# Short products ahead of groups of products in a two-part model on one core

## The reference

```python
# first block, for each layer l
x = layer_norm(ALPHA * x + 0.5 * swiglu(x, ffn_w1[l, 0], ffn_w2[l, 0]), ...)
x = layer_norm(ALPHA * x + hybrid_mixer(x, ...), ...)
x = layer_norm(ALPHA * x + 0.5 * swiglu(x, ffn_w1[l, 1], ffn_w2[l, 1]), ...)

def swiglu(x, w1, w2):             # w1: 1024 x 5632, w2: 2816 x 1024
    g, u = jnp.split(x @ w1, 2, axis=-1)
    return (jax.nn.silu(g) * u) @ w2

# second block: layer 0 is the even mixer (long convolution and attention),
# layer 1 the odd mixer: 8 recurrent heads (mLSTM) over 256 rows and 256 rows of context
q, k, v, o, z, gates = _split(h @ w_in, ODD_SPLITS)    # of each head: q, k 128 wide; v, o, z 256 wide
h = (h_f + h_b) * jax.nn.sigmoid(o)                    # a forward and a backward recurrence
return (rms_norm(h) * jax.nn.silu(z)) @ w_out
```

## Time and profile before

| | |
|---|---|
| median of 3 runs | 2158.39 us (2155.07 to 2162.65) |
| the profiled execution | 2157.61 us, span 2155.8 us |
| PE busy | 2124.5 us |
| DVE, ACT busy | 1428.7 us, 902.1 us |
| mean granted TensorE clock | 0.997 |

### The profile page before, as it was taken

The page is one execution under the profiler, slowest core; times in us unless marked ns, Lnnn a source line. Parts: engine busy times, 40 slices in busy tenths (PEclk is TensorE's granted clock), DMA queues, the critical chain, the costliest instruction groups (busy, mean ns, idle before and its releaser), DMA issues.

```text
span 2155.8 us, 35428 instructions
## 1 busy us (share of the span) xinstructions
PE 2124.5 (99%) x14996; PEld 1928.7 (89%) x14996; DVE 1428.7 (66%) x2066; ACT 902.1 (42%) x1066; POOL 18.7 (1%) x36
## 2 busy tenths in 40 slices
PE   9999999999999999999999999999999989999998
PEld 8998999999989989999899768888788879999996
DVE  5556878675566558876756767777666447665665
ACT  4343466344344434474434352222444344443442
POOL 0000000000000000000000000000000000000000
PEclk9999999999999999999999999999999999999999
DMA  9644555666566555555575422222212232332331
GB/s 363 225 178 190 196 196 215 235 235 254 196 265 234 190 190 196 196 196 215 196 247 216 177 80 79 79 79 79 79 40 79 88 117 79 118 118 79 118 118 59
DMA packets 29006, 349.56 MB, mean 162 GB/s; under 512 B 2993, under 2 KB 5425, under 8 KB 8369
## 3 DMA queue, kind: packets, MB, share of 16 engines
q1 hardware_dynamic: 24672, 313.42, 39.6%
q0 software_dynamic: 4176, 33.89, 4.1%
HBM read 346.24 MB, written 1.05 MB: 161 GB/s over the span
## 4 chain that ended last, share of the span: by engine, by line
PE 94%; DVE 2%; ACT 2%; DVEq 1%; ACTq 0%; issue 0%
PE banks L922 13%; PE banks L780 12%; PE banks L775 12%; PE banks L776 12%; PE banks L1009 8%; PE banks L1087 6%; PE banks L1084 6%; PE banks L1083 6%; PE banks L792 3%; PE banks L1101 2%; PE banks L1097 2%; PE banks L1098 2%; PE banks L1278 2%; PE banks L1277 2%; PE banks L1279 2%; PE banks L878 1%
## 5 line engine op out<-in xcount | busy, mean ns | idle before, releaser
L2101 DVE TENSOR_TENSOR w_lo<-ring,w_hi 128x2048 fp32r<-128x2048 f32 x290 | 661.9, 2289 | 391.7 <-ACT w_hi L1515 388.1
L1515 ACT ACTIVATE w_hi<-ring 128x2048 fp32r<-128x2048 f32 x290 | 555.9, 1918 | 675.6 <-PE banks L780 445.2
L775 PE MATMUL banks<-x_hi,w_hi 128*128 128x256 f32 x2112 | 497.0, 278 | 0.5 <-ACT w_hi L1515 0.5
L776 PE MATMUL banks<-x_lo,w_hi 128*128 128x256 f32 x2112 | 495.7, 277 | 0.0
L775 PEld LDWEIGHTS banks<-x_hi,w_hi 128*128 128x128 f32 x2112 | 397.2, 188 | 1.5 <-issue 1.5
L776 PEld LDWEIGHTS banks<-x_lo,w_hi 128*128 128x128 f32 x2112 | 397.3, 188 | 0.0
L780 PE MATMUL banks<-x_hi,w_lo 128*128 128x256 f32 x2112 | 284.6, 277 | 1.0 <-DVE w_lo L2101 1.0
L780 PEld LDWEIGHTS banks<-x_hi,w_lo 128*128 128x128 f32 x2112 | 260.7, 188 | 1.4 <-DVE w_lo L2101 1.4
L1083 PE MATMUL banks<-x_hi,w_hi 128*128 128x512 f32 (+1 forms) x656 | 232.7, 368 | 0.0
L1084 PE MATMUL banks<-x_lo,w_hi 128*128 128x512 f32 (+1 forms) x656 | 225.8, 358 | 0.0
L1552 ACT ACTIVATE arena<-banks 128x512 f32<-128x512 f32 (+5 forms) x178 | 79.7, 471 | 284.5 <-PE banks L1087 164.7
(11 more groups left out here) (378 smaller groups left out, 2806.0 us busy)
## 6 DMA issues: line engine op xcount, KB each, us to landing
ring<-weights SPq DMA_DIRECT2D x147, 2048.0 KB, 7.8
arena<-mods POOLq DMA_DIRECT2D x11, 2048.0 KB, 11.4
bcast<-lnrows POOLq DMA_DIRECT2D x12, 512.0 KB, 5.1
ring<-weights SPq DMA_DIRECT2D x2, 1024.0 KB, 9.9
filt_sb<-filt POOLq DMA_DIRECT2D x2, 609.0 KB, 22.4
xrow<-x SPq DMA_DIRECT2D x1, 1024.0 KB, 5.2
arena<-hy_consts POOLq DMA_DIRECT2D x1, 1024.0 KB, 13.0
xrow<-ctx_rows POOLq DMA_DIRECT2D x1, 1024.0 KB, 6.8
```

The costliest lines, as they stand in the source:

```text
L775: nc.tensor.matmul(out, hi[:, k, t * P:(t + 1) * P], x_h[:, k, :], start=k == 0, stop=False)
L776: nc.tensor.matmul(out, hi[:, k, t * P:(t + 1) * P], x_l[:, k, :], start=False, stop=False)
L1515: nc.scalar.activation(hi, raw, ACT.Copy).then_inc(w_hi_done, 1)
L2101: v.tensor_tensor(lo, raw, hi.bitcast(F32), ALU.subtract).then_inc(w_lo_done, 1)
```

## The change

`columns_half`, `tile_r`, `pair`, `value_tile` and `output_gates` get a number of columns, `first` (or `leads`, one for each side). Where it isn't 0, `lead` issues one product of the group's first stationary tile with the first columns of its first moving tile, into the place that the group then overwrites with `start=True`. It adds nothing to any result. It stands behind the group's waits for its bank and its high weights. There are 42: 8 in pairs 7 to 10 of the up stage (0, 0), 20 in pairs 1 to 10 of (1, 1), 7 ahead of the first of four value tiles (of heads 1 to 7) and 7 ahead of the first of two output gates (heads 1 to 7), of 8 to 256 columns each.

```diff
--- before.py
+++ after.py
@@ -133,6 +133,11 @@
 MOD_SETS = ((0,), (1, 2), (3,), (4,), (5, 6), (7,), (8, 9), (10,), (11,))
 MOD_SLOT = (0, 1, 0, 0, 0, 1, 0, 0, 1, 0, 0)
 MOD_BLOCK = {key[2]: n for key, n in BLOCK_OF.items() if key[1] == "mod"}
+UP_LEADS = {(0, 0, 7): (64, 128), (0, 0, 8): (192, 256), (0, 0, 9): (64, 128), (0, 0, 10): (192, 256)}
+UP_LEADS.update({(1, 1, j): (32 * j - 32 + 16, 32 * j) for j in range(1, 9)})
+UP_LEADS.update({(1, 1, 9): (8, 24), (1, 1, 10): (40, 56)})
+VALUE_LEADS = (32, 64, 96, 128, 160, 192, 256)
+GATE_LEADS = (0, 64, 128, 192, 256, 32, 96, 160)
 MOD_AT = 4
 FIRST_BANKS = (5, 6)
 FIRST_HALVES = HALF_OF[DEPTH, "hy", 0, 0]
@@ -762,13 +767,19 @@
                 else:
                     released(pe, (split - 1) // 3, "layer", "turn", (split - 1) % 3, b)
 
-            def columns_half(l, x_h, x_l, *key):
+            def lead(out, stationary, moving, n):
+
+                nc.tensor.matmul(out[:, 0:n], stationary, moving[:, 0:n], start=True, stop=True)
+
+            def columns_half(l, x_h, x_l, *key, first=0):
 
 
                 h = HALF_OF[(l,) + key]
                 b = take(pe, l, "layer", *key)
                 _, hi, lo = half_views(h)
                 hi_ready(h)
+                if first:
+                    lead(banks[:, b, 0:SEQ], hi[:, 0, 0:P], x_h[:, 0, :], first)
                 for t in range(2):
                     out = banks[:, b, t * SEQ:(t + 1) * SEQ]
                     for k in range(KT):
@@ -830,12 +841,12 @@
                         low_features(side, False)
                         low_weights(side, True)
 
-            def pair(l, x_h, x_l, *key, split=None):
+            def pair(l, x_h, x_l, *key, split=None, leads=(0, 0)):
                 if split is not None:
                     first_pair(l, x_h, x_l, *key, split=split)
                     return
                 for side in range(2):
-                    columns_half(l, x_h, x_l, *key, side)
+                    columns_half(l, x_h, x_l, *key, side, first=leads[side])
 
             def gates(l):
 
@@ -983,7 +994,8 @@
 
             def ffn(l, f):
                 for j in range(FJ):
-                    pair(l, x_hi, x_lo, "up", f, j, split=None if j else l * 3 + 2 * f)
+                    pair(l, x_hi, x_lo, "up", f, j, split=None if j else l * 3 + 2 * f,
+                         leads=UP_LEADS.get((l, f, j), (0, 0)))
                     if j == 0 and l + f:
                         mod_columns(MOD_GROUPS.index((l, "turn", 1) if f else (l - 1, "turn", 2)))
                     if (l, "up", f) in MOD_GROUPS:
@@ -1087,12 +1099,14 @@
                     mm = nc.tensor.matmul(out, lo[:, k, part_], x2_hi[:, k, cols_], start=False, stop=k == KT - 1)
                 return mm
 
-            def tile_r(out, h, r):
+            def tile_r(out, h, r, first=0):
 
 
                 _, hi, lo = half_views(h)
                 rows_ = slice(r * P, (r + 1) * P)
                 hi_ready(h)
+                if first:
+                    lead(out, x2_hi[:, 0, rows_], hi[:, 0, :], first)
                 for k in range(KT):
                     nc.tensor.matmul(out, x2_hi[:, k, rows_], hi[:, k, :], start=k == 0, stop=False)
                     nc.tensor.matmul(out, x2_lo[:, k, rows_], hi[:, k, :], start=False, stop=False)
@@ -1377,16 +1391,17 @@
                 b = take(pe, i, "ml", "k")
                 tile_t(banks[:, b, :], HALF_OF[DEPTH, "qkv", i, 0], 1).then_inc(full[b], 1)
 
-            def value_tile(i, r):
+            def value_tile(i, r, first=0):
                 b = take(pe, i, "ml", "v", r // 2) if r % 2 == 0 else plan["ml"]["v", r // 2][0]
-                mm = tile_r(banks[:, b, (r % 2) * 256:(r % 2 + 1) * 256], HALF_OF[DEPTH, "qkv", i, 1], r)
+                mm = tile_r(banks[:, b, (r % 2) * 256:(r % 2 + 1) * 256], HALF_OF[DEPTH, "qkv", i, 1], r, first)
                 if r % 2:
                     mm.then_inc(full[b], 1)
 
-            def output_gates(i):
+            def output_gates(i, first=0):
                 b = take(pe, i, "ml", "o")
                 for r in range(RT):
-                    mm = tile_r(banks[:, b, r * ML_V:(r + 1) * ML_V], HALF_OF[DEPTH, "oz", i, 0], r)
+                    mm = tile_r(banks[:, b, r * ML_V:(r + 1) * ML_V], HALF_OF[DEPTH, "oz", i, 0], r,
+                                first if r == 0 else 0)
                 mm.then_inc(full[b], 1)
                 b = take(pe, i, "ml", "z")
                 for t in range(2):
@@ -1433,7 +1448,7 @@
 
             for i in range(ML_HEADS):
                 if i:
-                    output_gates(i)
+                    output_gates(i, GATE_LEADS[i])
 
                 b = take(pe, i, "ml", "mb")
                 for d, c0 in ((0, SEQ), (1, 0)):
@@ -1470,7 +1485,7 @@
 
                 if i + 1 < ML_HEADS:
                     for r in range(4):
-                        value_tile(i + 1, r)
+                        value_tile(i + 1, r, 0 if r else VALUE_LEADS[i])
                 else:
                     odd_half(0, 1)
                     odd_half(1, 0)
```

## The result

The changed kernel takes 2166.57 us (median of 10 runs, 2162.51 to 2170.32) against 2158.33 us before (10 runs): 8.2 us more, ratio 1.0041 (95% interval 1.003 to 1.0052). A second set of 12 runs gave 1.0026 (1.001 to 1.0043). The forecast was 2158, with a range from 2152 to 2166. Both intervals exclude no change.

What follows compares the result with a forecast made beforehand. The prediction took PE (TensorE), busy 2124.5 of 2155.8 us, as the bound. Leads cost 4.75 us, quicker pace returns 5.4: -0.6 us; 2157.61 - 0.6 + 0.8 = 2157.8, said as 2158, range 2152 to 2166.

Steps and rivals of the forecast that it cites:

- the lower end: Price of a lead read from one-column products (L1009), 101 ns each: 4.2 us for 42 leads.
- The plain-fp32 rival: At the leads: short products go at 1.69 ns a column, costing 8.2 us; 2166.6 without pace answer; chance 0.18.
- Which value I take: Pace behind leads: three quarters of column groups quicker, 5.4 us back, heads nothing; with 4.75 us cost, sum -0.6 us.
- its zero: Starting point: up stages (0, 0) and (1, 1) at 117.8 ns before the change; quicker pace would give 5.97 us.
- the 6 in 8: Column groups behind the transposes of `mod_columns`: a restart ends at the quicker pace in 6 of 8 cases.
- three quarters forecast: Column groups behind leads: three quarters at the quicker pace, 0.75 x (5.97 + 1.17) = 5.4 us given back.
- its 1.17 us: Down stage behind (0, 0): 60.43 us instead of 61.60 if the quicker pace comes, a gain of 1.17 us.
- 14 of 14: Recurrent heads: all 14 restarts of value tiles and output gates ended at the slower pace, so no gain was taken.
- no answer: Whole kernel: the pace does not respond to leads, so their 4.75 us stands in full, 2163.1 us; chance 0.27.

Runs made afterwards that it cites:

- all_256: The changed kernel with all 42 leads made 256 columns wide, the width of the products behind them; 2164.59 us, ratio 1.0029.
- only_00: The changed kernel with only the eight leads of up stage (0, 0), all other leads 0; 2161.70 us, ratio 1.0007.
- pin_64: The kernel before plus thirteen leads of 64 columns, only where stretches of column groups begin; 2178.62 us, ratio 1.0084.
- pin_columns: The kernel before plus eight leads behind `mod_columns`, 64 columns at (0, 0) pair 7 and 16 elsewhere; 2159.00 us against 2157.88, ratio 1.0004.
- same_again: The kernel before, run again without an edit; 2162.35 us, ratio 1.0005.

## Why the prediction was wrong

**What held.** No wait swallows a lead. Its price is one slot at every width from 8 to 256 columns: 0.113 us was forecast, 0.114 to 0.12 measured in `all_256`, and the distances behind narrower leads add up to the same. (The eight one-column records from which the lower end was read are four products, two records each as in the earlier trace rows; the 101 ns are those of a record, and a lead is one record.) The plain-fp32 rival, whose 2166.6 is within 0.1 us of the result, is not what happened, and the agreement is luck: at its rate a lead of 192 columns would take some 320 ns, and it is 0.09 us from the lead to the next product. The pace does answer to leads, in column groups.

**The step that failed** is "Which value I take", in two terms. The larger one is its zero, 4.6 us (45.31, 61.69 and 113.15 in the first trace against the means 44.47, 61.10 and 109.97 of the table below). The forecast took (0, 0) and (1, 1) of the one trace, both slow, for what the kernel does in every execution, and counted every quick group as a gain. They were two draws that had come out slow. The rows it rested on said so: six of eight restarts were quick, so on the average these stretches too should have been taken as mostly quick already. Ten traces now hold 68 such stretches without a lead behind the transposes; 10 of them are slow, all at four of the eight places ((0, 0) pair 7, (0, 1) pair 1, (1, 0) pair 7, (1, 1) pair 1). The forecast used the 6 in 8 for the changed kernel and not for the kernel before.

The smaller term is the share of quick groups behind leads, three quarters forecast and 10 of 28 found, in every traced execution the same ten: 10 x 0.21 = 2.1 us instead of 5.4, 3.3 less. A lead is not one more restart of the kind in the earlier trace rows: what comes out depends on its width and on what stood before.

The sum put right, from the traces with and without leads at each stage (us):

| stage | without leads | mean | with leads | difference |
|---|---|---|---|---|
| (0, 0) pairs 7 to 10 | 45.31, 45.31, 43.63, 43.61 | 44.47 | 45.82 | +1.4 |
| down stage behind | 61.69, 61.69, 60.52, 60.52 | 61.10 | 61.69 | +0.6 |
| (1, 1) pairs 1 to 10 | 113.15, 108.90, 108.91, 108.91 | 109.97 | 113.80 | +3.8 |
| heads | 281.95, 281.96 | 281.95 | 283.98 | +2.0 |

Together 7.8 us, against 8.2 measured (interval 6.5 to 11.2) and 5.6 in the second set (2.2 to 9.3). Of the 7.8, some 4.9 are slots; the pace, forecast to give back 5.4, took 2.9 more. The down stage did not gain its 1.17 us because the last leads of (0, 0), 192 and 256 columns, leave the slower pace standing. In the heads the forecast had 14 slots, 1.6 us; the other 0.4 are z tiles behind the gates, which three leads left at the slower pace, less one gate stretch that came up. The forecast had also taken the slower pace of the gates for fixed, 14 of 14; that was one execution's outcome in part. In `only_00`, which has no lead there, the gates of heads 2 to 7 are quick and all z tiles slow (gates and z tiles of head 2):

```profile
1882.54:1888.07 5.53, 5.53 (x51) 1.00 0.88 317
1888.07:1893.82 5.75, 5.75 (x51) 1.00 0.16 64
```

`pin_64` and `pin_columns` show the same. It costs the heads 0.2 us as a whole, so the sum stands; the value tiles are slow in every trace.

**The range.** Its upper end, 2166, came from the plain-fp32 rival; apart from that rival the highest case was no answer, 2163.1, the bare cost of the slots. That a lead can put a stretch at the slower pace which would have been quick, 0.21 us for each group of 48, was mentioned and not priced: 18 groups x 0.21 = 3.8 us. This rival, leads fixing the slow pace, was missing.

**What stays open.** Four draws a stage are few, so the means in the table may be off by a us or so each. Why a stream of products has two paces, why the outcome repeats in threes with 64 columns, and why the value tiles always go at the slower one, no run here shows.

## What to carry to other kernels

Before an edit is credited with curing a slow stretch, see a second trace of the unedited kernel: what one execution did slowly, the next may do at full pace, and the median of the runs holds the mixture. A short product inside a saturated stream of load and product costs a whole slot of the stream, however narrow. An inserted instruction can fix a state that was random, and one that fixes the worse one costs more than itself: 1.5 us of leads made 18 us of time.

## What had not been expected of the hardware

A stretch of products of 256 columns in the fp32r format keeps one of two distances, 113.3 or 117.8 ns, at a granted clock of 1.00, until something breaks the stream; 0.2 us of transposes are break enough, the boundary between groups is not. A lead of the full 256 columns within a stretch changes nothing, 26 of 26 in `all_256`. All 42 leads of the changed kernel gave the same outcome in each of the three traces that hold them, while breaks without a lead come out either way; only where the stretch ahead was itself a draw did one lead differ between kernels (64 columns at (0, 0) pair 7). And the granted clock falls to 0.50, the 1.2 GHz level, early in some executions (13.65 us in the changed kernel, 14.3 us in `same_again`) and not in others. PE had been idle for 2.29 us just before 13.56 us in the changed kernel, and for as long just before 13.05 us in the kernel before, where the clock stayed at 1.00. There the same stretch (below) holds 32 products instead of 17, so the fall cost an estimated 1.7 us:

```profile
13.65:17.06 3.41, 3.41 (x32) 1.00 1.01 413
```
